# First two tiles finished by pairs of heads instead of by whole tiles, in a two-layer streaming encoder with a gathered-expert layer

## The reference, cut to what matters

```
x += W_out( concat[ poolmix, conformer_conv, gated_shortconv ] )(rms_norm(x) @ w_in)     # the mixer
x += peer(rms_norm(x))                                                                    # the experts

q      = (t @ w_q)                        -> 8 heads x 2 halves of 64
s      = q . sub_keys                     -> 128 scores per head and half; top 16 of each
cand   = sums of the two halves' top 16   -> 256 per head; top 16 of these
ids    = 128 * i + j                      -> 16 experts of 16384, per head and token
gates  = softmax(best 16 scores)          # per head
act    = gelu( t . expert_u[ids] )        # 128 rows of 1024 numbers per token
out    = sum( gates * act * expert_v[ids] )
```

## Time and profile before

| what | value |
|---|---|
| time, median of 3 runs | 3111.84 us (3108.88 to 3113.34) |
| the profiled execution | 3111.86 us, its span 3109.8 us |
| busy share PE, DVE, POOL, ACT | 70%, 70%, 66%, 9% |
| bytes moved | 1201.35 MB, mean 386 GB/s |
| gathered rows' queue (q0) | 1140.99 MB, 93.1% of 16 engines' span |

### The profile page before, as it was taken

The page is one execution under the profiler, slowest core; times in us unless marked ns, Lnnn a source line. Parts: engine busy times, 40 slices in busy tenths (PEclk is TensorE's granted clock), DMA queues, the critical chain, the costliest instruction groups (busy, mean ns, idle before and its releaser), DMA issues.

```text
span 3109.8 us, 23586 instructions
## 1 busy us (share of the span) xinstructions
PE 2183.4 (70%) x7198; PEld 752.9 (24%) x7198; DVE 2168.4 (70%) x5644; ACT 268.8 (9%) x515; POOL 2047.4 (66%) x2184
## 2 busy tenths in 40 slices
PE   7231797568877975488976376858997638675599
PEld 6211222222222221122322122312332212110122
DVE  4899378996777786727279997883718999646500
ACT  3010110100001000010110100101011010000000
POOL 0357467767777775566767677777676767767675
PEclk9665898779988988799988688969998868887799
DMA  6589899999999999999999999999999999999998
GB/s 251 200 315 410 313 370 409 409 410 408 387 409 408 400 410 411 399 405 386 409 371 395 395 400 408 409 402 410 388 410 364 405 392 409 410 401 410 400 410 346
DMA packets 331689, 1201.35 MB, mean 386 GB/s; under 512 B 40994, under 2 KB 41386, under 8 KB 329514
## 3 DMA queue, kind: packets, MB, share of 16 engines
q0 software_dynamic: 313344, 1140.99, 93.1%
q1 hardware_dynamic: 17130, 49.94, 4.2%
q10 hardware_dynamic: 1088, 8.91, 0.7%
HBM read 1188.82 MB, written 10.87 MB: 386 GB/s over the span
## 4 chain that ended last, share of the span: by engine, by line
PE 29%; DVE 23%; DMA 21%; POOL 19%; issue 8%; ACT 1%; ACTq 0%; DVEq 0%; POOLq 0%
POOL rows L617 19%; PE acc L1013 19%; DMA rows<-in_expert_v,idsT 16%; DVE rows L1461 9%; DMA rows<-in_expert_u,ids 3%; PE psA L828 3%; DVE psB L1189 2%; PE psB L956 2%; PE psA L881 2%; DVE work L1276 1%; DVE work L1269 1%; DVE work L1266 1%; PE psB L864 1%; DMA w_in_sb<-in_w_in 1%; DVE work L1310 1%
## 5 line engine op out<-in xcount | busy, mean ns | idle before, releaser
L1013 PE MATMUL acc<-rows,strip 128*32 128x512 f32 x4352 | 1411.8, 639 | 426.0 <-DMA rows<-in_expert_v,idsT 400.9
L1461 DVE CUSTOM_DVE_ANT_0 rows<-rows,psH 128x1024 f32<-128x1024 f32 x1088 | 1289.0, 1218 | 290.9 <-DMA rows<-in_expert_u,ids 268.0
L617 POOL DMA_INDIRECT rows<-in_expert_u,ids x1088 | 1020.1, 938 | 566.4 <-issue 299.7
L617 POOL DMA_INDIRECT rows<-in_expert_v,idsT x1088 | 1026.2, 943 | 473.0 <-issue 299.9
L1013 PEld LDWEIGHTS acc<-rows,strip 128*32 128x32 f32 x4352 | 335.9, 113 | 1407.9 <-issue 742.0
L828 PE MATMUL psA<-w_out_sb,hT 128*128 128x512 f32 x320 | 165.4, 663 | 55.1 <-ACTq L694 39.7
L1189 DVE SCALAR_TENSOR_TENSOR psB<-zbuf,chan,psB 128x128 f32<-128x128 f32 (+1 forms) x841 | 201.8, 329 | 1.7 <-DVE work L1212 1.2
L1468 DVE TENSOR_TENSOR x_out<-acc,x_out 128x1024 f32<-128x1024 f32 x10 | 12.2, 1222 | 239.1 <-PE acc L1013 238.6
L864 PE MATMUL psB<-w_in_sb,hT 128*128 128x512 f32 x288 | 140.8, 638 | 48.5 <-DVE hT L1170 48.5
L956 PE MATMUL psB<-w_q_sb,hT 128*128 128x512 f32 x288 | 141.1, 640 | 32.8 <-DVE hT L1170 32.8
L881 PE MATMUL psA<-w_in_sb,hT 128*128 128x512 f32 x288 | 132.4, 607 | 0.0
(11 more groups left out here) (185 smaller groups left out, 1338.4 us busy)
## 6 DMA issues: line engine op xcount, KB each, us to landing
rows<-in_expert_u,ids POOLq DMA_INDIRECT x1088
rows<-in_expert_v,idsT POOLq DMA_INDIRECT x1088
w_in_sb<-in_w_in ACTq DMA_DIRECT2D x4, 2176.0 KB, 18.1
w_in_sb<-in_w_in SPq DMA_DIRECT2D x4, 2176.0 KB, 23.4
w_out_sb<-in_w_out SPq DMA_DIRECT2D x2, 4096.0 KB, 19.0
w_q_sb<-in_w_q SPq DMA_DIRECT2D x2, 4096.0 KB, 24.9
x_out<-x_mid SPq DMA_DIRECT2D x10, 512.0 KB
x_mid<-x_mix SPq DMA_DIRECT2D x8, 512.0 KB, 6.7
```

The source lines that it names most:

```text
L617: nc.gpsimd.indirect_dma_start(out=rows[:, j, :], out_offset=None, in_=table[:, :], in_offset=bass.IndirectOffsetOnAxis(ap=index, axis=0))\
L1013: last = nc.tensor.matmul(acc[LS * a:LS * (a + 1), half:half + 512], strip[:, first:first + LS], rows[:, at % RING, half:half + 512], star ...
L1461: nc.vector.tensor_tensor_reduce(rows[:, j, :], rows[:, j, :], psH[:, :], 1.0, 0.0, ALU.mult, ALU.add, dots[:, r:r + 1]).then_inc(s_free[j ...
```

## The change

The item's 128 picks are treated as four quarters (a quarter is a pair of heads, 32 picks) for items 0 and 1.

- Item 0: only pair 0 is routed in the prologue. Pairs 1 to 3 are routed in ticks 0 to 5 of superstep 0, between u rows (`first_routing`). Each pair has its own logits, exponent, softmax and turned ids. Three v rows stand in the list of fetches before the last u row of quarter 0.
- Items 0 and 1: GELU, weighing and turning are done per quarter, at the ticks of `GELU_AT`. `coefT` now holds, for 32 picks, another arrangement: partition 32q + k, column t is pick k of token 4t + q, so laying out takes four copies per group, one for each band q, and the v rows of a quarter can be added as soon as that quarter is done.
- A v row i of items 0 and 1 is thus no longer all picks of one token: row i belongs to quarter i // 32, and carries 32 picks of four tokens.
- All 128 v rows of item 0 are taken in superstep 0; 96 of item 1 in superstep 1, the other 32 in superstep 2. From `FETCHES` entry 696 on (counted from 0; the first u row of item 3) the list is the same as before.
- The scores of pairs 2 and 3 of item 0 are copied from `psB` to `x_out`, and `x_out` of item 0 is loaded at tick 36 of superstep 0 instead of tick 10 of superstep 1; its sum moves from tick 27 to tick 2 of superstep 1.
- PE takes v rows in chunks of 4 everywhere, 8 in tick 5 of superstep 0.

Cut to its core (line marks left out; the semaphore counts that follow from quarters are left out too):

```diff
-EARLY = {ROUTE + 5: (0, 12), ROUTE + 8: (12, 24)}
-TAKEN = 24
+QUARTERS = 4
+QUARTERED = 2
+GELU_AT = ((4, 6, 14, 27), (8, 16, 21, 27))
+U_QUARTERS = ([8] * 4 + [16] * 2 + [6, 6, 1, 1, 1, 1, 8, 8] + [2] * 8 + [3, 3, 4, 3, 3],
+              [4] * 8 + [2, 2, 2, 2, 8, 8, 4, 4] + [4, 6, 6, 8, 8] + [5, 5, 5, 6, 6, 5])
+V_CLOSE = [2, 3, 3, 4, 4, 4] + [4] * 6 + [2] * 3
+V_QUARTERS = ([0] * 5 + [32, 0, 2, 5, 5, 5, 5, 1, 1, 0, 2, 2, 1, 1, 1, 1, 2, 2, 2, 3, 3, 2] + V_CLOSE,
+              [0] * 9 + [6, 6, 6, 2, 2, 2, 2, 0, 2, 1, 2, 1, 2, 2, 2, 3, 3, 2] + V_CLOSE)
+PARKED = 3
...
-V_PLAN = {0: [(10, 42, 0, 0, 96)], 1: [(0, 25, 0, 96, 128), (29, 42, 1, 0, 56)],
-          2: [(0, 25, 1, 56, 128), (29, 42, 2, 0, 56)],
+V_PLAN = {0: [(0, 42, 0, 0, 128)], 1: [(0, 42, 1, 0, 96)],
+          2: [(0, 25, 1, 96, 128), (29, 42, 2, 0, 56)],
...
-X_PLAN = [("sum", 0, (1, 10), (1, 27)), ("sum", 1, (2, 10), (2, 27)), ("sum", 2, (3, 10), (3, 36)),
+X_PLAN = [("sum", 0, (0, 36), (1, 2)), ("sum", 1, (2, 10), (2, 27)), ("sum", 2, (3, 10), (3, 36)),
...
+    def opening():
+        first, second = ([key for tick in ticks for key in u_at(0, tick)] for ticks in (range(4), range(4, 6)))
+        some = [key for tick in range(6) for key in v_at(0, tick)]
+        return first[:-PARKED - 1] + merged(first[-PARKED - 1:], some[:PARKED]) + merged(second, some[PARKED:])
+    FETCHES = opening() + [key for n in range(ITEMS + 1) for tick in range(0 if n else 6, TICKS)
+                           for key in merged(u_at(n, tick), v_at(n, tick))]
...
-        return i % 4, i // 4
+        return i % 4, i % LS // 4 if v < QUARTERED else i // 4
+    def index_column(v, i):
+        a, b = place(v, i)
+        return SPICK * (i // LS) + 8 * a + b if v < QUARTERED else per_band(v) * a + b
...
+        def laid_off(q):
+            turn, o = divmod(LS - 1 + q, LS)
+            return strip[:, LS * turn:LS * (turn + HALVES)].rearrange("p (s o) -> p s o", o=LS)[:, :, o]
...
+        ids_turned = [psA[:, 0:LS], acc[:, 0:LS], psA[:, 0:LS], psA[:, 512:512 + LS]]
+        between, last_place = psB[:, 768:768 + LS], psH[:, 0:LS]
+        coef_turned = [[acc[:, 512:512 + LS], psA[:, 0:LS], between, last_place], [between] * 3 + [last_place]]
...
-                        pool.wait_ge(s_idsT, m + 1)
-                    a, b = place(m, i)
-                    t = per_band(m) * a + b
+                    if m == 0 and i % LS == 0:
+                        pool.wait_ge(s_idsT, upto(0, i // LS))
+                    elif i == 0:
+                        pool.wait_ge(s_idsT, upto(m))
+                    t = index_column(m, i)
...
+            def keep_quarter(n, part):
+                act.wait_ge(s_cturn, weighed(n, part))
+                nc.scalar.copy(coefT[:, n, LS * part:LS * (part + 1)], coef_turned[n][part]).then_inc(s_cT, 1)
+            def keep_scores():
+                act.wait_ge(s_sc2, 1)
+                act.wait_ge(s_k1st, 16)
+                nc.scalar.copy(x_out[:, :], psB[:, :]).then_inc(s_sck, 1)
+            def lay_out_quarter(v, g):
+                part, g4 = divmod(g, LS // GROUP)
+                k = GROUPS.index((v, g))
+                act.wait_ge(s_cT, weighed(v, part))
+                if k >= 2:
+                    u, ahead = GROUPS[k - 2]
+                    done(act, ("v", u, GROUP * (ahead + 1) - 1))
+                for q in range(COPIES):
+                    r = slice(q * LS, (q + 1) * LS)
+                    dst = laid_off(q)[r, k % 2 * GROUP:(k % 2 + 1) * GROUP].rearrange("p (b a) -> p b a", a=4)
+                    src = coefT[r, v, LS * part:LS * (part + 1)].rearrange("p (a b) -> p b a", a=4)
+                    step(nc.scalar.copy(dst, src[:, 2 * g4:2 * g4 + 2, :]))
+                settle()
+                act.sem_inc(s_strip, 1)
...
+            keep_scores()
+            exponents(0, 0)
             for n in range(ITEMS + 2):
                 for tick in range(TICKS):
+                    if (n, tick) == (0, 3):
+                        exponents(0, 1)
+                    if (n, tick) == (0, 5):
+                        exponents(0, 2)
+                        exponents(0, 3)
+                    for part in weighed_at(n, tick):
+                        gelu_of(n, part)
+                        keep_quarter(n, part)
...
+            def turn_quarter(out, in_, part):
+                for q in range(COPIES):
+                    last = nc.tensor.matmul(out[q * LS:(q + 1) * LS, :], in_[:, SPICK * part:SPICK * (part + 1)],
+                                            ident[:, :].rearrange("p (j q) -> p q j", q=COPIES)[:, q, :],
+                                            start=True, stop=True)
+                return last
+            def turn_quarter_ids(part):
+                pe.wait_ge(s_idf, upto(0, part))
+                turn_quarter(ids_turned[part], idf[0], part).then_inc(s_iT, 1)
+            def turn_quarter_coefficients(n, part):
+                pe.wait_ge(s_coef, weighed(n, part))
+                if (n, part) == (0, 1):
+                    pe.wait_ge(s_idsT, upto(0, 2))
+                turn_quarter(coef_turned[n][part], coef, part).then_inc(s_cturn, 1)
...
+            turn_quarter_ids(0)
             for n in range(ITEMS + 1):
                 for tick in range(TICKS):
+                    if (n, tick) == (0, 5):
+                        turn_quarter_ids(1)
+                    if (n, tick) == (0, 6):
+                        turn_quarter_ids(2)
+                        turn_quarter_ids(3)
+                    if (n, tick) == (0, GELU_AT[0][0] + 1):
+                        turn_quarter_coefficients(0, 0)
+                    for part in weighed_at(n, tick):
+                        if part and not (n, tick) == (0, GELU_AT[0][0]):
+                            turn_quarter_coefficients(n, part)
                     for v in ended(n, tick, TURN):
                         turn_coefficients(v)
                     if tick == TURN_H and n + 1 < ITEMS:
                         turn_h(n + 1)
                     tokens = v_at(n, tick)
-                    some = 2 if u_at(n, tick) else 4
+                    some = 8 if (n, tick) == (0, 5) else 4
...
+            def first_routing(tick):
+                if tick == 0:
+                    turned_quarter(0)
+                    softmax(0, 0)
+                    yield from top_keys(0, 1)
+                if tick == 1:
+                    yield from top_sums(0, 1)
+                if tick == 2:
+                    yield from experts(0, 1)
+                    logits(0, 1)
+                if tick in (4, 5):
+                    pair = tick - 2
+                    if pair == 2:
+                        yield
+                        yield
+                        weigh(0, 0)
+                        turned_quarter(1)
+                        softmax(0, 1)
+                        yield
+                    yield from top_keys(0, pair)
+                    yield
+                    yield from top_sums(0, pair)
+                    yield
+                    yield from experts(0, pair)
+                    logits(0, pair)
+                if tick == 6:
+                    weigh(0, 1)
+                    for part in (2, 3):
+                        turned_quarter(part)
+                        softmax(0, part)
+                        yield
...
-            for tick in range(CENTRE, TICKS):
+            for tick in range(CENTRE, ROUTE + 3):
                 for _ in mixer(0, tick):
                     pass
-                for r in range(*EARLY.get(tick, (0, 0))):
-                    take_row(0, r)
+            logits(0, 0)
             for n in range(ITEMS + 2):
...
-                    picked = taken_at(n, tick)
+                    picked = u_at(n, tick)
+                    for part in weighed_at(n, tick):
+                        if n or part > 1:
+                            for _ in range(2):
+                                if picked:
+                                    take_row(n, picked.pop(0)[2])
+                            weigh(n, part)
+                    if n == 0:
+                        for _ in first_routing(tick):
+                            if picked:
+                                take_row(n, picked.pop(0)[2])
                     if n + 1 < ITEMS:
```

More of the change, by code:

```diff
@@ L208, in ended, with weighed_at @@
     def ended(n, tick, ago):
-        return [n] if n < ITEMS and tick == U_END[n] + (ago if n else AT_ONCE[ago]) else []
+        return [n] if QUARTERED <= n < ITEMS and tick == U_END[n] + ago else []
+    def weighed_at(n, tick):
+        return [p for p in range(QUARTERS) if n < QUARTERED and tick == GELU_AT[n][p]]
     def loads_at(n, tick):
@@ L1333, in experts, with logits @@
                 dve.sem_inc(s_ids, 1)
[L1335 to L1337 removed]
+            def logits(m, part=0):
+                cols = columns(m, part, 1)
+                heads = (cols.stop - cols.start) // TOPK
+                b3 = best[:, cols].rearrange("p (h k) -> p h k", k=TOPK)
```

134 lines of the change are left out of this document (83 added, 51 removed).

## The result

| | before | after |
|---|---|---|
| median of 4 runs (us) | 3112.59 (3108.88 to 3114.57) | **3067.57** (3066.18 to 3069.43) |
| ratio to before | 1 | 0.9855 [0.9843, 0.9867] |
| profiled execution, its span | 3111.86, 3109.8 | 3068.15, 3066.2 |

The changed kernel is 45.0 us faster by the medians and 43.6 us by the spans of the two profiled executions. On one of the chips used further on, one execution of control_b (3473.69 us, granted clock 0.611) and one of the kernel before (3615.83 us, 0.566) fell into a second, slower state of the chip, and the medians given there leave them out.

What follows compares the result with a forecast made beforehand. The DMA stream of gathered rows was taken to bound the kernel. Winning 55.4 us of empty DMA time, less 10 us at the parked rows and 4 us in superstep 1, takes 3111.86 to 3070 us, range 3050 to 3098.

Steps and rivals of the forecast that it cites:

- The prize: Empty DMA time in tile 0, 105 to 200 and 300 to 420 us: at most 55.4 us to win back.
- (1): Start of superstep 0, routing between dot products: DVE through 32 rows at 162 us, DMA full up to there.
- (2): Parked expert_v rows of tile 0: v0's buffer released at 170 us, DMA idle 10 us, bounds 3 and 20.
- (3): Ticks 4 and 5 of superstep 0: even race of DVE and DMA, 69 us each; price 0, up to 5.
- (4): Rest of superstep 0: DVE is not the bound, the 300 to 420 us loss goes; price 0 of 0 to 10.
- (5): Superstep 1, hand-off of tile 1's first quarter: DVE 4.5 us behind; 4 us lost, bounds 0 and 8.
- (6): Queues of ACT, PE, SP and POOL: extra layouts, table changes, turns, chunks and loads cost 0; PE between -5 and +5.
- Table change on a hand-off: ACT's table switch: by the skill's rule 1.38 us of drain beside the 1.28 us load, making the total 3072.
- A: Rival: PE and DVE serving one ring in superstep 0 lose more, 20 us at the parked rows; 3090, chance 0.2.
- C: Rival: the quarters' eight hand-offs each stop the ring, 7 us or more apiece decides; slower, 3124 at 8.5, chance 0.06.
- B: Rival: everything fits, only a 3 us restart at the parked rows and superstep 2's 6.3 us gained; 3053, chance 0.1.
- D: Rival: PE's chain sets supersteps 3 to 9, so the early lead vanishes later; 3112, chance 0.04.

Runs made afterwards that it cites:

- control_b: The changed kernel unaltered, on a chip with a slower stream: 3352.26 us, ratio 0.9901 to the kernel before.
- control: The changed kernel unaltered, run again as the base for other runs: 3067.01 us, ratio 0.9852 to the kernel before.
- parked0: The changed kernel with no expert_v row parked ahead, the first one (v0) at place 33 of the fetches instead of 29: 3061.75 us.
- parked5: The changed kernel with five expert_v rows parked ahead instead of three, the first one (v0) at place 27 instead of 29: 3070.95 us.
- chunks2: The changed kernel with PE taking two expert_v rows a chunk in ticks with u rows (superstep 0's tick 5 keeps eight): 3068.22 us.
- before_chunks4: The kernel before with PE taking four v rows a chunk everywhere, on a slow-stream chip: 3382.60 us, ratio 0.9994 to the kernel before.
- Late_v: The changed kernel with no row parked and v0 at place 35 instead of 29, on a slow-stream chip: 3343.10 us, ratio 0.9879 to before.
- late_both: The changed kernel with v0 at place 35 and tile 1's first v row 7 instead of 3 places behind its 32nd u row: 3064.93 us.

## Why the prediction was right

The forecast was 3070 and the kernel takes 3067.6; by the two profiled executions -43.6 us against -41.4. It is the likeliest case that came, not a rival, and by its steps:

- **The prize**, 29.6 + 25.8 us: both stretches were won, less what is named below. 300 to 420 us moves 406 GB/s, as said (405 or more).
- **(1)** DVE through 32 rows at 162 us: 164.02. The stream began 2.3 us later (107.56 for 105.28 us), so the steps from there are right to under 1 us. DMA was full from 120 to 160 us (409 GB/s); from 115 on it is 405, for the 410 that was named as a sign, as the later start reaches into 115 to 120 us (377).
- **(2)** v0 given back at 170 us: 170.79; stream idle for 10 us: 9.1 (control 8.6). The sum held, but not by its parts. Counted from the start of the stream, the release was to come 8 us after DVE's last row and came 6.8 us after it. My terms as they stand (2.5 + 2.3 + 2 + 1.85) give 8.65 us at full clock and up to 10.5 at half, so that 170 had been rounded down; what they really took was 2.2 us for the two dot products, 1.8 for weighing, turning, keeping and the first layout, 0.6 for w_in and 2.2 up to the release. The four records of w_in run beside the copies (166.70 to 168.68) and not behind them, and the clock that I had taken at the 1.2 GHz level is 1.00 from 160 to 175 us, the 2.4 GHz level, after PE had been given 16 records of w_in at 154.95 us. The restart, taken as 3 us from the first start, is seen in the windows after the release: 167 GB/s from 170.8 to 175 us and 302 from 175 to 180 us, (410 - 167)/410 x 4.2 + (410 - 302)/410 x 5 = 3.8 us. A shorter path, a later start and a longer restart met in a good total, and that is luck. Parked0 and parked5 confirm the mechanism, not only the size: the hole follows v0's place. The window after the release:

```profile
170.80:175.00 4.20, 1.46 (x8) 0.26 (x4) 1.74 (x10) 0.00 (x0) 3.29 (x4) 1.00 0.56 167
```

- **(3)** ticks 4 and 5, 0 us: 0.5 us of 105 to 200 us lies outside the first 10 us and the hole, nearly all of it in 115 to 120 us, and 200 to 300 us lost 0.2. An even race, and it cost nothing.
- **(4)** the rest of superstep 0, 0 us taken out of 0 to 10: 1.2 us.
- **(5)** superstep 1, 4 us: 3.2 - 0.6 = 2.6 us more is lost there than before, at the place that was named, the hand-off of tile 1's first quarter (2.8 us in control). The place was right: the GELU waits for DVE's dot products until 502.18 us, and from there to PE's first expert_v rows at 510.01 it takes 7.8 us, at the upper end of the 5 to 8 that I had for a hand-off; the wait is put down to PE. Of its reason one half is borne out. The 32nd u row went out at 485.64 us and, with the page's 10.9 us from issue to landing, lay there at about 496.5 (an estimate); its dot product began at 500.92, so DVE was some 4.4 us behind, as I had reckoned. But the weighed coefficients, ready at 504.53, then stood until PE came out of the mixer's matmuls and turned them at 508.40, 3.9 of the 7.8 us, and for PE's order of work the sum had no term. Superstep 2's 6.3 us, "moved, not gained", became 4.0: 2.3 us gained. The last stage gained 1.3 us more, less than its rounding.
- **(6)** queues and chunks, 0: chunks2 and before_chunks4 show the chunks' part as 0. ACT's layouts (it still waits 658.2 us before the line of the later tiles) and SP's loads were not tried by themselves, and the table by stages can't rule them out, as it shows where the stream stood and not for whom. Between the first fetch and 740 us every POOL wait over 3 us is put down to PE's use of rows, for which ACT's layouts may or may not have been late; that is all that is known.
- **Table change on a hand-off**: the exponent's table is loaded at 108.72 us for 1.28 us, with DVE idle for 1.99 us until the softmax at 110.28; the whole softmax took 3.9 us, for which I had said 4. By the rule in the Trainium skill (ScalarE: Activation LUTs, What ACT_TABLE_LOAD costs) another 1.38 us of drain would stand beside it; no such gap is in this trace, in which ACT's copy before the load ends at 108.70 us and the exponent starts at 110.01. The first line below is ACT's, the second DVE's, which waited for it:

```profile
108.72 1.28 ACT L755 ACT_TABLE_LOAD   x1
...
110.28 0.19 DVE L1491 TENSOR_REDUCE hsum<-best 128x2 f32<-128x32 f32 x1 [1.99 <-ACT best L755]
```

The terms: -55.4 + 9.1 (for 10) + 2.6 (for 4) + 1.2 (for 0) - 2.3 - 1.3 (superstep 2 and the rest, for 0) + 2.2 (a later start, for 0) + 0.7 (what remains up to 300 us) = -43.2 us. Errors of 1 to 2 us on both sides met in the sum; the total is nearer than its parts had a right to.

**Checkpoints.** One missed: the first dot product of tile 1 was to come at 450 and came at 459.56. The stream kept the sum: place 256, that dot product's row, went out at 444.32 us. DVE did not. I had let the row be taken when it came, but the routing of tile 1, some 59 us of DVE without a pause in both kernels, stands between tile 0's last u row and this one. It began at 400.54 us before, behind a wait on PE, and at 395.41 after, behind the last u row's dot product (389.25, which had waited for DMA) and 4.76 us for ACT's GELU:

```profile
389.25 1.22 DVE L1627 CUSTOM_DVE_ANT_0 rows<-rows,psH 128x1024 f32<-128x1024 f32 x1 [1.33 <-DMA rows<-in_expert_u,ids]
...
395.25 0.19 DVE L1619 TENSOR_TENSOR gates<-dots,gates 128x32 f32<-128x32 f32 x1 [4.76 <-ACT dots L760]
```

```profile
400.54 0.89 DVE L1263 MAX8 work<-psB 128x8 f32<-128x128 f32 x4 [28.60 <-PE psA L982]
```

The stream meanwhile ran on out of v rows (409 GB/s from 420 to 480 us). It was a bad mark for the lead; fetch 697, said for 1027, went out at 1028.63, and was a good one. The longest POOL wait before 740 us is the hole's own, and the next in after are 4.90 and 4.86 us. But in control one of 5.90 us stands at 512 us, over the 5 us that I gave as a sign of rivals A and C; it cost 2.8 us, and neither rival came.

**The rivals.** A (3090) wanted 20 us at the parked rows; the worst order tried, parked5, has 11.2. B (3053) had the hole at the restart alone: parked0 comes to 3.0 us and 3061.75, so B's mechanism exists, only not in this order of rows. C wanted eight stops of 7 us and more; one such is in after. D wanted the lead to vanish: 39 us of it at place 696, 44 at the end.

**What stays open.** Late_v alone was not run at 409 GB/s; by late_both's 160 to 200 us (2.8 us lost, 3.2 in parked0) it would be less than 1 us below parked0, an estimate. Of the versions that ran, **parked0 is the best, 3061.75 us**, and beats both kernels. How much tile 1's quarters are worth at 409 GB/s was not measured; on the slow-stream chip it is at most 26 us. Why the gain is smaller there, 30.9 us, is seen only in part: control_b's superstep 1 runs at 348 GB/s where before_chunks4's has 368, with a lead of 35.6 us at place 256 and of 19.9 at 340, and POOL waits of 9.96 us on DVE at place 294 and 7.61 us on PE at place 303. Why rows come more slowly there was not looked into. The traces of those chips have POOL waits put down to "remote", 329.7 us in 246 waits in control_b, of which control and after have none; what stands behind the name is not shown.

## What to carry to other kernels

When one stream bounds a kernel, book each stage by what the stream left unused; the change's gain, its new costs and what is still to be had then stand in one column. That it closes (here to 0.4 us of 43.6) follows from equal bytes and proves no cause; the cause has to come from a run, as that of the parked rows did. In a ring of buffers that is taken in turn and emptied by two engines, place a row so that its consumer is ready when the ring comes round to it: each place too early cost 1.4 us here, and a place that is late for one consumer may put the other's rows in front of a long piece of its own work. Spreading the producers' work alone brought 13 and 18 us on two chips, where the whole change brought 31 on the first of them; the rest wants rows of the other kind to fetch in the meantime.

## What the runs showed of the hardware that was not expected

The same two kernels on other chips: 3384 us where 3112 was seen, with the gathered stream at some 368 GB/s (DMA share 0.96) instead of 409 to 410 (1.03), while TensorE's granted clock was hardly different (means of 0.81 to 0.84 for the kernels there, 0.86 for control). The one comparison made on both, the changed kernel against the one before, kept its sign and not its size: 45.6 us of gain became 30.9. And the prologue, which no kernel here changes, ended at different times: the first fetch went out between 105.1 and 108.0 us over fourteen traces, which alone moves a single execution by more than some of the differences looked for, so those rest on medians of several runs.
